# A three-layer transformer block on one core: wide experts in whole fp32, and a weight ring of twelve places

## The reference

```
x = x + token_mixer(rms_norm(x));  x = x + moe_one(rms_norm(x));  x = rms_norm(x)
for layer in (0, 1):                                    # "wide" layers
    mix = even_mixer(x) if layer == 0 else fourier_mixer(x)
    x = layer_norm(ALPHA * x + mix)
    x = layer_norm(ALPHA * x + moe_2(x))
```

## Time and profile before

| what | value |
|---|---|
| three runs | 2005.18, 2002.22, 2004.66 us |
| the profiled execution's own time | 2002.44 us |
| its span, first to last instruction | 2000.5 us |
| PE busy | 1785.5 us (89%) |
| DVE, ACT, POOL busy | 674.3, 427.7, 83.4 us |
| mean granted clock of PE | 0.951 of full |
| moved by DMA | 581 MB, 291 GB/s over the span |
| wide layer 0, first gate product to last down product | 994 to 1432 us |
| wide layer 1, the same | 1541 to 1979 us |
| narrow layer, first gate product | 565 us |

### The profile page before, as it was taken

The page is one execution under the profiler, slowest core; times in us unless marked ns, Lnnn a source line. Parts: engine busy times, 40 slices in busy tenths (PEclk is TensorE's granted clock), DMA queues, the critical chain, the costliest instruction groups (busy, mean ns, idle before and its releaser), DMA issues. The chain is left out here.

```text
span 2000.5 us, 20692 instructions
## 1 busy us (share of the span) xinstructions
PE 1785.5 (89%) x8544; PEld 952.9 (48%) x8544; DVE 674.3 (34%) x1347; ACT 427.7 (21%) x713; POOL 83.4 (4%) x66
## 2 busy tenths in 40 slices
PE   7999897895799999799799999899597999998995
PEld 6884454695455555456434443333254344442331
DVE  3657333446223334443412222122303122221223
ACT  2321224352222221222211111111112111111110
POOL 0000001311100000120100000000001000000000
PEclk9999998797899999899799999999897999999998
DMA  5345320004669996432999999999793999999995
GB/s 194 127 162 178 123 88 4 0 1 194 243 249 398 403 419 266 144 155 73 384 423 423 423 423 423 423 424 423 299 375 143 424 423 423 423 423 424 423 423 232
DMA packets 100017, 581.49 MB, mean 291 GB/s; under 512 B 23947, under 2 KB 26251, under 8 KB 34893
## 3 DMA queue, kind: packets, MB, share of 16 engines
q1 hardware_dynamic: 87997, 577.81, 70.8%
q10 hardware_dynamic: 11920, 2.26, 0.6%
HBM read 577.39 MB, written 2.62 MB: 290 GB/s over the span
## 5 line engine op out<-in xcount | busy, mean ns | idle before, releaser
L1717 PE MATMUL up_ps_l<-pool,hT 128*64 128x512 f32 x640 | 143.5, 597 | 13.4 <-DMA pool<-in_expert_w_up 13.4
L1717 PE MATMUL gate_ps_l<-pool,hT 128*64 128x512 f32 x640 | 141.4, 593 | 6.6 <-DMA pool<-in_expert_w_gate 5.3
L446 PE MATMUL proj_ps<-pool,hT 128*128 128x512 f32 x320 | 140.2, 598 | 5.6 <-DVE pool L684 5.6
L1740 PE MATMUL y_ps_l<-pool,hidden_l 128*64 128x512 f32 x640 | 142.6, 596 | 2.3 <-ACT hidden_l L1803 1.4
L1870 DVE SCALAR_TENSOR_TENSOR y_low_l<-y_ps_l,slot_gate_l,y_high_l 128x512 fp32r<-128x512 f32 x64 | 47.1, 751 | 251.2 <-ACT y_high_l L1813 251.2
L438 PE MATMUL proj_ps<-hT,pool 128*128 128x256 f32 x512 | 111.9, 380 | 0.0
L1860 DVE TENSOR_TENSOR hidden_l<-hidden_l,up_ps_l 128x512 f32<-128x512 f32 x32 | 22.0, 688 | 245.2 <-PE up_ps_l L1717 245.2
L438 PEld LDWEIGHTS proj_ps<-hT,pool 128*128 128x128 f32 x512 | 96.9, 190 | 14.8 <-issue 1.8
L446 PEld LDWEIGHTS proj_ps<-pool,hT 128*128 128x128 f32 x320 | 61.4, 192 | 81.3 <-issue 74.7
L1717 PEld LDWEIGHTS gate_ps_l<-pool,hT 128*64 128x64 f32 x640 | 45.5, 137 | 98.4 <-issue 87.6
L1717 PEld LDWEIGHTS up_ps_l<-pool,hT 128*64 128x64 f32 x640 | 43.6, 137 | 99.4 <-issue 77.8
(11 more groups left out here) (503 smaller groups left out, 2682.0 us busy)
## 6 DMA issues: line engine op xcount, KB each, us to landing
pool<-in_expert_w_gate SPq DMA_DIRECT2D x40, 2048.0 KB, 32.4
pool<-in_expert_w_up SPq DMA_DIRECT2D x40, 2048.0 KB, 30.2
pool<-in_expert_w_down SPq DMA_DIRECT2D x40, 2048.0 KB, 32.1
pool<-in_w_in_blocks SPq DMA_DIRECT2D x18, 2048.0 KB, 7.7
pool<-in_moe_w_gate SPq DMA_DIRECT2D x12, 2048.0 KB, 12.6
pool<-in_moe_w_up SPq DMA_DIRECT2D x12, 2048.0 KB, 12.0
pool<-in_moe_w_down SPq DMA_DIRECT2D x12, 2048.0 KB, 11.6
gate_room<-in_expert_w_gate SPq DMA_DIRECT2D x12, 2048.0 KB, 29.9
```

The source lines that it names most:

```text
L446: last = mm(pp[:, n % 2, j * W:(j + 1) * W], k.hT[:, c, j * P:(j + 1) * P], wbuf[n % 2][:, c, :], start=(c == 0), stop=(c == KC - 1))
L1717: last = mm(out[e * CAP:(e + 1) * CAP, 0:H], xg(part * r + c)[:, at:at + CAP], ex.weights(i, e, c), start=(part + c == 0), stop=(part == e ...
L1740: last = mm(Y[e * CAP:(e + 1) * CAP, n], hidT[:, part * r + c, e * CAP:(e + 1) * CAP], ex.weights(i, e, c)[:, n * W:(n + 1) * W], start=(p ...
```

## The change

Eight edits, of which the first four touch the wide experts:

1. Wide experts: no split. The gather takes x itself in fp32 with an fp32 one-hot, one product where there were two; `y_high` is the whole result in fp32, `y_low` and its VectorE operation are gone, and a scatter part is one fp32 product. ScalarE's `h_high` and GpSimd's `h_low` are no longer made in the wide layers. As x must stay unchanged for later gathers, the adds go to a second pair of rows, `k.sum`, and the two are swapped behind the stage.
2. Batches: the first is a single pair in both kinds of layer. Behind it a batch is 4 pairs for the narrow experts, as before, and 1 pair (before: 2) for the wide ones.
3. Order in a pair: scatter part 0 (and 1 where a gather follows) stands ahead of up, the others up to 2 behind up, then the first two groups of the gather, the turned hidden rows, the rest of the gather, and part 3, which now has up's bank and waits for no add of its own pair. Gate waits group by group for the gathered rows.
4. Ring of the wide experts: 12 places (`first_room` and `second_room` are new). Three chunks of layer 0 are issued at the end of the even layer's SP program (`early`), two of them when the 8th and 10th half product free their places. Then 7 and 2 in `stage_out_route`. For layer 1 it is 3, 5, 2 and 2.
5. The narrow experts keep the split and the 8 places.
6. `stage_norm_t`, which was only called without a weight, becomes `stage_turn`.
7. Gains, biases and temporaries are carved from rooms that are free.
8. `stage_general` (not run with these inputs) reads x the new way.

```diff
@@ ring and batches
-RING = 10
+RING = 12
-    def __init__(self, k, before, tag, H, batch, w_gate, w_up, w_down):
+    def __init__(self, k, before, tag, H, batch, split, w_gate, w_up, w_down):
+        self.batches = [[0]] + [list(range(p, min(p + batch, NE // 2))) for p in range(1, NE // 2, batch)]
...
+    per = [4 // len(b) for b in ex.batches]
+    groups = [KC // n for n in per]
...
-        scatter_bank = [XG[:, 0], XG[:, 1], SC[:], XG[:, 0]]
+        scatter_bank = [XG[:, 0], XG[:, 1], SC[:], Up[:]]
+        def early(p):
+            return 2 if new_batch(p) else 1
@@ gather
-                                moving = one[:, j].rearrange("p e s -> p (e s)")
-                                mm(at, k.h_high[:, j, c], moving, start=(j == 0), stop=False)
-                                last = mm(at, k.h_low[:, j, c], moving, start=False, stop=(j == NJ - 1))
+                                moving = one[:, j].rearrange("p e s -> p (e s)")[:, 0:width]
+                                if ex.split:
+                                    mm(at, k.h_high[:, j, c], moving, start=(j == 0), stop=False)
+                                    last = mm(at, k.h_low[:, j, c], moving, start=False, stop=(j == NJ - 1))
+                                else:
+                                    last = mm(at, k.x[:, j, c:D:KC], moving, start=(j == 0), stop=(j == NJ - 1))
@@ scatter
-                    if o == 3:
-                        pe.wait_ge(s_add, 4 * p + 1)
-                    mm(scatter_bank[o], to_tile, yh[:, o % 2], start=True, stop=False)
-                    mm(scatter_bank[o], to_tile, yl[:, o % 2], start=False, stop=True).then_inc(s_sc, 1)
+                    last = mm(scatter_bank[o], to_tile, yh[:, o % 2], start=True, stop=not ex.split)
+                    if ex.split:
+                        last = mm(scatter_bank[o], to_tile, yl[:, o % 2], start=False, stop=True)
+                    last.then_inc(s_sc, 1)
@@ a pair on the tensor engine
+                    if p:
+                        pe.wait_ge(s_y_ready, 2 * p)
+                        pe.wait_ge(s_add, 4 * p - 4)
+                        for o in range(early(p)):
+                            scatter(p - 1, o)
                     hidden(p, 1, Up)
                     if p:
-                        pe.wait_ge(s_ys, 2 * p)
-                        if p > 1:
-                            pe.wait_ge(s_add, 4 * p - 4)
-                        scatter(p - 1, 0)
-                        scatter(p - 1, 1)
+                        for o in range(early(p), 3):
+                            scatter(p - 1, o)
+                    if b:
+                        if p:
+                            pe.wait_ge(s_add, 4 * p - 2)
+                        gather(b, 0, 2)
                     pe.wait_ge(s_hid, p + 1)
...
                     last.then_inc(s_ht, 1)
+                    if b:
+                        gather(b, 2, groups[b])
                     if p:
-                        scatter(p - 1, 2)
                         scatter(p - 1, 3)
-                    if new_batch(p):
-                        if p:
-                            pe.wait_ge(s_add, 4 * p)
-                        gather(p // GB + 1)
@@ no high and low rows in the wide layers
                 def high(j):
+                    if bias is not None:
+                        return
...
-                for j in range(NJ):
+                for j in range(NJ if bias is None else 0):
                     pool.wait_ge(s_hi, j + 1)
@@ loads
+        def early(sp, s_half):
+            ex[1].load(sp, 1)
+            for products in (8, 10):
+                sp.wait_ge(s_half, products)
+                ex[1].load(sp, 1)
...
-            ex[2].load(sp, 2)
+            ex[2].load(sp, 3)
...
-                stage_fourier(k, lambda sp: ex[2].load(sp, 4))
+                stage_fourier(k, lambda sp: ex[2].load(sp, 5))
...
-                ex[1 + n].load(sp, 2 if n else 8)
+                ex[1 + n].load(sp, 2 if n else 7)
```

More of the change, by code:

```diff
@@ L252, in stage_first, with stage_turn @@
     k.scope = k.ctx
-def stage_norm_t(k, tag, src, weight, ahead=None):
+def stage_turn(k, src, ahead):
     nc = k.nc
-    s_w, s_ss, s_inv, s_rs, s_h, s_t = (k.sem(f"{n}_{tag}") for n in (
-        "norm_weight_loaded", "sumsq_done", "inv_done", "rstd_done", "h_done", "turned"))
+    s_t = k.sem("mixer_turned")
     scope = ExitStack()
     k.scope = scope
[L262 to L269, removed]
+    turned = k.ps("turned_ps_mixer", [P, 4, W])
     with scope, nc.Block() as block:
@@ L273, in _ @@
         def _(sp):
[L274 to L281, removed]
-                for j in range(NJ):
[L283 to L286, removed]
+            ahead(sp)
         @block.vector
         def _(dve):
[L290 to L298, removed]
-                    nc.vector.scalar_tensor_tensor(out=rows[:, j, :], in0=src[:, j, :], scalar=rstd[:, j:j + 1],
-                                                   in1=wrow[:], op0=ALU.mult, op1=ALU.mult).then_inc(s_h, 1)
             for b in range(4):
@@ L1629, in stage_experts @@
     with k.nc.Else():
-        stage_general(k, ex.tag + "g", ex.H, *ex.dram)
+        stage_general(k, ex, ex.tag + "g", ex.H, *ex.dram)
 def stage_packed(k, ex, alpha, ahead=None):
     nc = k.nc
-    tag, H, HT, GB = ex.tag, ex.H, ex.HT, ex.batch
+    tag, H, HT, GB = ex.tag, ex.H, ex.HT, ex.widest
     NI = NE // 2
     CP = len(ex.of_pair)
-    PER = 4 // GB
+    DT = F32R if ex.split else F32
+    per = [4 // len(b) for b in ex.batches]
+    groups = [KC // n for n in per]
+    groups_before = [sum(groups[0:n]) for n in range(len(groups) + 1)]
     (s_pm, s_gx, s_xg, s_sg, s_hid, s_pg, s_pt, s_one, s_slot, s_ht, s_hts, s_y, s_yh, s_ys,
@@ L2065, with stage_even @@
 RD = 128
-def stage_even(k):
+def stage_even(k, early):
     nc, i = k.nc, k.i
@@ L2512, in build @@
         ex[0].ring(k.store, 2)
-        for n in range(2):
-            ex[1 + n].ring(k.pool, 6)
         rows_pc, rows_cp = "(p c) n -> p c n", "(c p) n -> p c n"
-        def split_rows(tag):
-            k.h_high, k.h_low = (k.sb(f"h_{n}_{tag}", [P, NJ, KC, P], F32R) for n in ("high", "low"))
         with ExitStack() as mixer:
@@ L2538, in build @@
             k.scope = even
-            k.w_even0 = k.sb("w_even0", [P, KC, W])
-            k.norm_f_row = k.sb("norm_f_row", [P, D])
+            k.w_even0 = k.carve(k.gate_room, 0, [P, KC, W])
+            k.norm_f_row = k.carve(k.gate_room, CHUNK, [P, D])
+            k.sum = k.x
             with ExitStack() as packed:
                 k.ctx = k.scope = packed
-                split_rows("one")
+                k.h_high, k.h_low = (k.sb(f"h_{n}", [P, NJ, KC, P], F32R) for n in ("high", "low"))
                 def rest(sp, s_out):
```

208 lines of the change are left out of this document (116 added, 92 removed).

## The result

The changed kernel takes 2156.83 us, the median of 4 runs (2153.74 to 2160.32), against 2004.45 for the kernel before on the same chip: 1.0763 times as long, interval 1.0741 to 1.0785. Forecast were 2045 and a range of 2025 to 2066. The direction was right, the size was not: +42.5 expected, about +152 measured. The profiled run has a span of 2151.8 us, 151.3 more than before.

A forecast was written before the change was run, and what follows sets the result against it. Tensor engine work was taken to bound each wide layer first, the DMA its end. Two wide layers at +20.6 (+41.2) and the narrow experts' +1.3 gave +42.5 on 2002.44 us, so 2045, range 2025 to 2066.

The forecast's parts named there:

- Gather: Wide experts: 32 fp32 records a pair at 0.116 us, 3.7 (up to 4.6) us a pair instead of 2.0.
- (C): Rival: waits inside a wide pair grow, gather at 0.144 a record, 30.35 us a pair, 2079 us in all; 9%.
- The slack: Wide layers: the tensor engine has 23 us a layer, 1.45 us a pair, of waits for chunks.
- The scatter: Wide experts: four whole fp32 products take 3.8 us a pair instead of 2.12, +1.7.
- The bound: Wide layers after the change: no product waits for a DMA; a middle pair takes 29.15 us against the DMA's 29.75.
- Early loads: Chunks loaded ahead of the wide layers could land the last 14.9 and 9.9 us sooner, but are worth nothing.
- The start of a wide layer: Before the first gate: -1.3 with h_low gone, -0.3 smaller one-hot, -0.7 group-wise waits; together -2.3 us a layer.
- The end of a wide layer: Last scatter: half the 1.57 wait for y_low goes (-0.75), fp32 scatters add 1.5; together +0.7 us.
- The narrow experts: Narrow layer: gate 3.5 us sooner, four later gathers +3.5, fewer waits -0.7, ScalarE's copy +2; +1.3, between -3 and +5.
- (A): Rival: pairs under about 26.9 us, transfers end both wide layers 14.9 and 9.9 us sooner, 1978 us; 4%.
- (B): Rival: whole fp32 costs per record what the split costs, 27.7 us a pair, about 2000 us, no change; 3%.
- (D): Rival: up stalls on a late add, as the third scatter's bank is now up's; no chance of its own.

The follow-up runs named there:

- e1: The changed kernel with the wide gather reading 128 neighbouring columns of x instead of every eighth (other columns than needed): 2032.49 us, 1.0166 of the kernel before.
- e8: The changed kernel with x packed by ScalarE once a layer, so the wide gather reads side by side, and adds made in place: 2034.51 us, 1.017.
- e6: The kernel before with only the wide scatter in whole fp32, y_low gone: 2004.88 us, 1.0017.
- e7: The changed kernel without the three early chunks in the even layer, its twelve places kept: 2153.74 us, 1.0767.
- f2: e8 with the scatter split into fp32r high and low again and eleven ring places, early loads kept: 1995.3 us, 0.9969 of before.
- f3: f2 with ten ring places and without the early loads: 1997.94 us, 0.998.
- e3: The kernel before with h_high and h_low of the wide layers kept in row order and read with a step of 8: 2012.09 us, 1.0048.
- f5: The changed kernel with the kernel before's two-pair batches, high and low parts and ten places in wide layers, three early chunks kept: 2003.97 us, 1.0017 of before.
- e2: The changed kernel with the wide gather's stationary operand read at step 2 in layer 0 and 4 in layer 1: 2093.55 us, one run.
- e9: The changed kernel with the wide gather's stationary operand read at step 3 in layer 0 and 6 in layer 1: 2115.95 us, one run.
- e4: The changed kernel with wide batches of two pairs behind the first (256 moving columns) and eleven ring places: 2054.0 us, 1.0262.

## Why the prediction was wrong, and where it was right

**The failed step is "Gather".** It reads: "The nearest row, same type, shape and tile, has 3.7 / 32 = 0.116 a record". The row was nearest in all that the row shows, and it doesn't show the step of the stationary operand. The diff did: `c:D:KC`, with KC = 8, stood in the added line, and no operand of the earlier trace rows was compared with it. The runs put 0.241 in its place, 7.52 us a pair instead of 3.7. That the same record costs 0.12 with its numbers side by side (e1, e8) shows that the row itself was read rightly. With that one number a middle pair becomes 23.75 - 2.12 + 3.8 + 7.5 = 32.9 (measured 32.86). Fifteen pairs of a layer have a gather, 15 x 3.71 = 55.6 us more than forecast, which is what the layers show (77.8 instead of 22.2, and 77.3). Two layers are 111 us, and the forecast missed the span by 151.3 - 42.5 = 109.

**The range failed with it.** The bounds for the gather ran from 3.7 to 4.6 a pair, both ends from rows whose stationary numbers lie side by side, so rival (C), the highest, ended at 2079. No bound covered a property that the rows didn't share with the new instruction. The rest of the sum stood: with the reading mended, 2032.49 (e1) and 2034.51 (e8) lie 11 to 13 us under the forecast of 2045, inside the range.

**Right, each by its own row:** *The slack.* "That number decides the case" held: e6 put 25 us into 23 of slack and paid 3 in the kernel. (The prediction called all 23 waits for chunks; the profile of before lists 19 of them in layer 0.) *The scatter*, 3.8 forecast, 3.72 measured. *The bound*: no product of the wide layers waits for a DMA. *Early loads* worth nothing beside a full tensor engine (e7); that the twelve places are worth nothing either was not tested alone.

*The start of a wide layer*, -2.3 forecast, half of it arrived. One term did as forecast: the VectorE operation that took 1.49 beside GpSimd's h_low takes its neighbours' time once that is gone:

```profile
973.67 0.16 DVE L1478 TENSOR_REDUCE max_l<-logits_l 128x2 f32<-128x8 f32 x1
973.86 0.17 DVE L1479 TENSOR_TENSOR eq_l<-logits_l,max_l 128x8 f32<-128x8 f32 x1
```

Layer 0 starts 3.2 sooner, of which 2 come from ahead (the narrow layer ends 2.0 sooner), and layer 1's stretch is 1.3 shorter. So about 1.2 of the 2.3 arrived at each, since layer 1's first gather, from its first record to the gate behind it, takes 1613.94 - 1606.09 = 7.85 with its long loads instead of the 6.5 assumed. With the reading mended (e1, e8, f2, f3) the stretch from the narrow layer's last down to layer 0's first gate is 3.3 to 3.5 shorter than before, so the term was too small by 1. The window from 1606 to 1614 shows a granted clock of 0.65, and single records of this gather stand 0.240 apart at its start and 0.239 at its end. In e1 the records of the same gather stand 0.213 apart at first and 0.112 later: a lower clock lengthens the short load and not the long one.

*The end of a wide layer*, +0.7 forecast and +0.7 measured. The wait of 1.57 is halved:

```profile
2130.24 1.98 PE L1722 MATMUL gather_ps_l<-y_high_l,hT 128*128 128x512 f32 x4 [0.79 <-ACT y_high_l L1814]
```

*The narrow experts*, +1.3 forecast, about 0 measured: the last down starts at 797.99 instead of 799.96, but the stage's places were computed 2.15 sooner too. That head start is not the change's: in e3, whose narrow layer and earlier stages are those of before, the first gate comes 5.9 later than before, so the stages ahead vary by this much between executions. From the places to the last down the stage takes 0.2 us more than before. That the sum came near is partly luck, since its inside is less tidy. The first gather's records came out at the cheaper of my two prices, 0.21 for 128 columns like 256 ones at the low clock. It moved the gate by 4.0, though, and not by 5.3, since the clock never rose during it. And that it ended sooner bought only part of it, because the gate behind it then began at a lower clock:

```profile
559.15 3.68 PE L1714 MATMUL gate_ps_one<-pool,hT 128*64 128x256 f32 x16
562.62 2.46 PE L1714 MATMUL gate_ps_one<-pool,gate_room 128*64 128x256 f32 x16
565.01 0.44 PE L1753 MATMUL turn_ps_one<-tables,gate_room 128*128 128x128 f32 x2
```

The first half of gate takes 3.68 where the earlier trace rows has 1.95, both halves with their turn 2.2 more. The first half sits wholly in the low clock. In the window from 552 to 559 the granted clock is 0.50, the lower of the two levels (1.2 of 2.4 GHz), and from 559 to 565 it is 0.60; before, the window from 559 to 565 has 1.00.

**Rivals.** (A), where transfers set the end, had a flaw of its own beside its price for records. It let the last chunk land 14.9 us sooner for three early chunks; f5 shows with ten places that a lead is worth no more than there are free places to put it in. So (A) would have had to be worked out from two more places, not three chunks, in layer 0; no run has twelve places and a tensor engine that is fast enough. The Trainium skill, "TensorE: Matmul & The Clock Gate", section "Back-to-back issue gap", gives about 81 ns for 128 columns. No run here shows it: at full clock the records of a gather stand 0.11 apart at the least (e1, f5). (B), whole fp32 at the split's price, falls with the scatter's 0.45 a record and the gather's 0.241. (C) had the right place, the gather, and the right sign, but from a row of a stage at lower clock, so that it came nearest is luck; it had a third of the size, 34 us where 109 were missing. (D): up never waited for the bank of the third scatter.

**Left open.** The turns of x read it with a step of 8 as well, and they are spared: their records stand 0.11 apart at full clock, as those of the turned hidden rows do, and their loads are short (kernel before):

```profile
L1404 PEld LDWEIGHTS turned_ps_l<-tables,x 128*128 128x128 f32 x16 | 2.1, 190 | 1.0 <-issue 1.0
```

Which of the two operands the engine holds there isn't told by the trace, so what spares them wasn't settled; until it is, the price by step is shown for products alone. A ring of eleven with batches of two pairs and the split scatter, where (A) might come true, wasn't tried.

## What to carry to other kernels

When a price is taken from a row, compare the access pattern of its operands in the code too: type, shape and tile in the row were all equal here, and the step of the stationary operand made a factor of two. Work added to an engine with slack is paid only beyond the slack (e6: 25 us a layer for 3 in the kernel), and past it in full (the gather: about 121 of 123). A lead in transfers is worth no more than the free places that can hold it.

## What the runs showed of the hardware

- A record of a product with 128x128 stationary numbers in fp32 and 128 moving columns costs 0.12 us with the stationary numbers side by side (e1) and 0.13 with every second one (e2), 0.18 with every third (e9), 0.23 to 0.24 with every fourth, sixth and eighth (e2, e9, the changed kernel). In fp32r, with 256 columns, steps 1 and 8 cost the same 0.12 and 0.24 (e3). At the low clock step 8 stays at 0.24, while step 1 goes from 0.112 to 0.213, and doubling the moving columns to 256 adds only 0.013 to a record with step 8 (e4).
- An fp32r record of 128 columns costs as much as one of 256 at the low clock, 0.21 (narrow layer of the changed kernel), which fits a pace set by the load and not by the columns.
- A shorter first gather can leave the next product at a lower clock: in the narrow layer gate took 2.2 us more (granted clock 0.60 instead of 1.00) after a first gather that ended 4.0 sooner. This is one place in one profiled execution and was not tested apart.
